# MLP products by Strassen's scheme, with operands and block sums through DRAM, in a hybrid decoder step

## The reference, cut to what matters

```python
z = rmsnorm(x, g_pre_mix) @ w_in            # attention and recurrence follow from z
mix = concatenate([attn, o], -1) @ w_out    # 1024 x 1024
x = x + rmsnorm(mix, g_post_mix)
hid = square(relu(rmsnorm(x, g_pre_mlp) @ w_up))    # w_up 1024 x 4096
x = x + rmsnorm(hid @ w_down, g_post_mlp)           # w_down 4096 x 1024
```

## Time and profile before

| | |
|---|---|
| span of the profiled execution | 4277.1 us |
| median of the runs less that span | 1.6 us |
| PE busy | 3791.6 us, 89% |
| DVE busy | 2761.0 us, 65% |
| ACT busy | 2042.7 us, 48% |
| POOL busy | 381.2 us, 9% |
| everything ahead of the last stage | 0 to 2503 us |
| `attend_prompt` | 2006 to 2503 us |
| last stage, `output_and_mlp` | 2506 to 4277 us |

### The profile page before, as it was taken

The page is one execution under the profiler, slowest core; times in us unless marked ns, Lnnn a source line. Parts: engine busy times, 40 slices in busy tenths (PEclk is TensorE's granted clock), DMA queues, the critical chain, the costliest instruction groups (busy, mean ns, idle before and its releaser), DMA issues. The chain is left out here.

```text
span 4277.1 us, 52892 instructions
## 1 busy us (share of the span) xinstructions
PE 3791.6 (89%) x18920; PEld 3002.3 (70%) x18921; DVE 2761.0 (65%) x4534; ACT 2042.7 (48%) x3270; POOL 381.2 (9%) x390
## 2 busy tenths in 40 slices
PE   8999996779776589854999989999999999999998
PEld 7878775667555245432888877888888888877776
DVE  6686566888888798787788855434544454445444
ACT  3333324556677599875777742233223322331233
POOL 0000003545210111100100000000000000000000
PEclk9999998999877799985999999999999999999999
DMA  6555444225100344334111033323333342323222
GB/s 166 172 149 167 127 125 119 89 83 161 53 20 17 104 170 171 127 101 114 53 43 36 16 124 114 91 96 94 125 122 94 109 138 92 98 79 100 71 77 69
DMA packets 283783, 435.67 MB, mean 102 GB/s; under 512 B 86136, under 2 KB 154712, under 8 KB 275224
## 3 DMA queue, kind: packets, MB, share of 16 engines
q1 hardware_dynamic: 261256, 318.98, 25.3%
q0 software_dynamic: 21872, 113.52, 7.5%
q10 hardware_dynamic: 416, 0.02, 0.0%
HBM read 371.02 MB, written 61.43 MB: 101 GB/s over the span
## 5 line engine op out<-in xcount | busy, mean ns | idle before, releaser
L3140 DVE TENSOR_TENSOR weight_parts<-weights,weight_parts 128x1024 fp32r<-128x1024 f32 x280 | 344.9, 1233 | 769.3 <-ACT weight_parts L2939 769.3
L2939 ACT ACTIVATE weight_parts<-weights 128x1024 fp32r<-128x1024 f32 x280 | 296.0, 1059 | 976.5 <-PE acc L3517 460.7
L3517 PE MATMUL acc<-act_T,weight_parts 128*128 128x512 f32 x3072 | 707.8, 392 | 9.4 <-DVE act_T L3146 7.9
L3517 PEld LDWEIGHTS acc<-act_T,weight_parts 128*128 128x128 f32 x3072 | 580.6, 189 | 133.5 <-DVE act_T L3146 6.0
L3549 PE MATMUL acc<-weight_parts,hidden_parts 128*128 128x512 f32 x2304 | 522.7, 389 | 0.0
L3549 PEld LDWEIGHTS acc<-weight_parts,hidden_parts 128*128 128x128 f32 x2304 | 432.4, 188 | 89.8
L712 PE MATMUL accumulated<-hT,w_in_parts 128*128 128x512 f32 x1536 | 355.1, 390 | 0.0
L2651 DVE TENSOR_SCALAR_CACHE_REDUCE junk_dve<-score,candidate 128x2048 bf16<-128x2048 f32 (+6 forms) x224 | 328.5, 1505 | 8.8 <-DVE candidate L2637 8.2
L712 PEld LDWEIGHTS accumulated<-hT,w_in_parts 128*128 128x128 f32 x1536 | 287.0, 188 | 60.3
L2574 ACT ACTIVATE junk_act<-score,candidate 128x1920 bf16<-128x1920 f32 (+6 forms) x224 | 285.8, 1286 | 20.7 <-DVEq L2638 15.3
L330 ACT ACTIVATE w_in_parts<-w_in_raw 128x1024 fp32r<-128x1024 f32 (+1 forms) x112 | 113.6, 1014 | 307.8 <-PE accumulated L708 121.8
(11 more groups left out here) (502 smaller groups left out, 6915.0 us busy)
## 6 DMA issues: line engine op xcount, KB each, us to landing
weights<-in_w_up SPq DMA_DIRECT2D x128, 512.0 KB
weights<-in_w_down SPq DMA_DIRECT2D x128, 512.0 KB
w_in_raw<-in_w_in SPq DMA_DIRECT2D x80, 512.0 KB, 4.1
weights<-in_w_out SPq DMA_DIRECT2D x24, 512.0 KB
w_in_raw<-in_w_in SPq DMA_DIRECT2D x64, 128.0 KB, 2.7
q_rows<-scratch_qT SPq DMA_DIRECT2D x64, 128.0 KB, 3.6
qi_rows<-scratch_qiT SPq DMA_DIRECT2D x56, 128.0 KB
x_sb<-in_x_prompt POOLq DMA_DIRECT2D x3, 2048.0 KB, 9.3
```

The lines of the kernel that those rows point to most:

```text
L2939: act.activation(w2[:, w, 0, :], raw[:, b[0], :], ACT.Copy).then_inc(hi_rdy, 1)
L3140: dve.tensor_tensor(w2[:, w, 1, :], raw[:, b, :], w2[:, w, 0, :].bitcast(F32), ALU.subtract).then_inc(lo_rdy, 1)
L3517: mm = pe.matmul(acc[:, u % nb, :], w2[:, c % 2, b, k2 * ST + n * P:k2 * ST + (n + 1) * P], aT[:, a, 2 * kk + k2, :], start=(kk == 0 and k ...
```

## The change

`attend_prompt` gets a second job for POOL: 32 times it loads 1 MB of w_down (16 times) or w_up (16 times), forms four block sums of 128x512 each and stores them (1 MB) to DRAM, spread over the tiles from the fifth on (`WITH_TILE`). `output_and_mlp` is replaced by three stages.

`output_projection` takes 16 prompt tiles of 128 rows and the sample rows as a 17th: transposes, 48 matmuls, norm, residual, second norm, transposes back. It stores the residual rows, the transposed normed rows and, by POOL, their four block sums, to DRAM.

`mlp_up` takes two halves of 1024 tokens. In Strassen's scheme (the form with 7 products and 15 sums) a product of 2 x 2 blocks takes seven block products instead of eight. A unit is a pair of 128-column blocks of w_up: 7 products of 12 matmuls; there are 32 units, 2688 matmuls. The x operands (28 pieces of 256 KB for each half) and the weight operands (7 pieces of 256 KB for each unit) come from DRAM in pieces of 128x512 through 12 buffers. DVE adds the products out of PSUM, squares, POOL forms the sums of the hidden blocks for `mlp_down`, and SP stores 7 tensors of 256 KB for each unit, in runs of 512 bytes.

`mlp_down` has 2 x 7 x 4 = 56 steps of 48 matmuls (2688). A step loads 1 MB of hidden operand (POOL's queue) and converts it in two halves; a product (four steps) needs 16 weight pieces of 256 KB, which are loaded through four buffers and converted during its predecessor's last step. The sample rows' whole MLP is done here, as 128 pieces of weight (64 up, 64 down), two buffers deep: the high and low parts of the 64 rows stand side by side as one stationary operand of 128 columns, so a piece takes two matmuls, 256 in all, and a small product with `fold` adds the two halves.

"The last block as three blocks" means that a stage has taken the place of each part of it. `newton`, the conversion and `PASSES` are as before. Cut to what the prediction speaks of (new code in the four functions):

```diff
 def attend_prompt(nc, io, sc):
+        WITH_TILE = [0, 0, 0, 0, 1, 1, 2, 2, 2, 3, 3, 3, 4, 4, 4, 3]
+                def load_weights(c):
+                    if c >= 2:
+                        pool.wait_ge(sums_out[c % 2], 16 * (c // 2))
...
+                    pool.dma_start(t, src).then_inc(w_in[c % 2], 16)
+                def weight_sums(c):
+                    pool.wait_ge(w_in[c % 2], 16 * (c // 2 + 1))
...
+                        pool.tensor_tensor(s1, a21, a22, ALU.add).then_inc(sums_rdy, 1)
+                        pool.tensor_tensor(s3, a11, a21, ALU.subtract).then_inc(sums_rdy, 1)
+                    if 0 < c < 2 * FPAIRS - 1:
+                        load_weights(c + 1)
...
+                        pool.tensor_tensor(s2, s1, a11, ALU.subtract).then_inc(sums_rdy, 1)
+                        pool.wait_ge(sums_rdy, 4 * c + 3)
+                        pool.tensor_tensor(s4, a12, s2, ALU.subtract).then_inc(sums_rdy, 1)
...
+                    pool.dma_start(dst, wsum[:, (2 * c + 1) % 3, :].rearrange("p (s d) -> p s d", s=4)).then_inc(sums_out[c % 2], 16)
                 for i in range(NT):
                     b = i % 2
                     pool.wait_ge(q_hi, i + 1)
                     pool.tensor_tensor(qs[64:P, b, :, :], qr[64:P, b, :, :], qs[64:P, b, :, :].bitcast(F32),
                                        ALU.subtract).then_inc(q_lo, 1)
...
+                    for c in range(sum(WITH_TILE[:i]), sum(WITH_TILE[:i + 1])):
+                        weight_sums(c)
-def output_and_mlp(nc, io, sc):
+def output_projection(nc, io, sc):
...
+            def _(dve):
+                for n in range(TILES + 2):
+                    if n + 1 < TILES:
+                        mix_low(n + 1)
+                    if n >= 2:
+                        turned_out(n - 2)
...
+                    y = mean_and_root(n, 0, pt)
+                    dve.scalar_tensor_tensor(z, z, y, gpm[0:pt, :], ALU.mult, ALU.mult).then_inc(scaled, 1)
...
+                    dve.tensor_tensor(x, x, z, ALU.add).then_inc(x1_rdy, 1)
+                    y = mean_and_root(n, 1, pt)
...
+                    dve.tensor_scalar(hr[0:pt, n % 2, :], x, y, None, ALU.mult).then_inc(hr_rdy, 1)
+            def _(pe):
+                for n in range(TILES + 2):
+                    if n + 1 < TILES:
+                        turn_mix(n + 1)
+                    if n < TILES:
+                        pe.wait_ge(mix_lo, n + 1)
...
+                    if n >= 2:
+                        turn_rows(n - 2)
+def mlp_up(nc, io, sc):
+    RAW, SLOTS, AHEAD, BANKS = 12, NPROD, 5, 8
...
+                for n in range(-AHEAD, len(ready_at)):
+                    while n + AHEAD < len(ready_at) and done < ready_at[n + AHEAD]:
+                        low(done)
+                        done += 1
+                    if n >= 0:
+                        out_of_bank(n)
...
+                        for q in range(QUADS):
+                            for b, a in PASSES:
+                                mm = pe.matmul(acc[:, n % BANKS, :], wp[:, n % SLOTS, b, q * P:(q + 1) * P], XC[:, i, a, q, :],
+                                               start=(q == 0 and (a, b) == (0, 0)), stop=(q == QUADS - 1 and b == 1))
+def mlp_down(nc, io, sc):
+    A_RING, B_RAW, S_RING = 4, 4, 2
+    PERSTEP = 6
+    AFTER = (3, 5, 8, 10, 13, 15)
...
+                def load_b(m):
+                    if m >= B_RAW:
+                        sp.wait_ge(b_lo, m - B_RAW + 1)
...
+                def load_w(y):
+                    if y >= S_RING:
+                        sp.wait_ge(w_lo, y - S_RING + 1)
...
+                def a_high(s):
+                    for x in range(2):
+                        g = 2 * s + x
+                        act.wait_ge(a_in[g % A_RING], 16 * (g // A_RING + 1))
+                        if s >= 2:
+                            act.wait_ge(done, s - 1)
+                        act.activation(ap[:, g % A_RING, 0, :], araw[:, g % A_RING, :], ACT.Copy).then_inc(a_hi, 1)
...
+                for s, (h, i, r) in enumerate(STEPS):
+                    if s + 1 < len(STEPS):
+                        a_low(s + 1)
+                    if s:
+                        out_of_bank(s - 1)
+                        for n, h_, second, r_ in finished(s - 1):
+                            norm_rows(k, x_no, second, r_)
+                            k, x_no = k + 1, x_no + 1
+                    if r == LAST and (h, i) != (HALVES - 1, NPROD - 1):
+                        for kp in range(FPAIRS):
+                            b_low((NPROD * h + i + 1) * FPAIRS + kp)
+                    for y in sample_pieces(s):
+                        w_low(y)
...
+                    for kp in range(FPAIRS):
+                        x, j = divmod(kp, 8)
+                        g = 2 * s + x
+                        if j == 0:
+                            pe.wait_ge(a_lo, g + 1)
+                        if r == FIRST:
+                            pe.wait_ge(b_lo, (NPROD * h + i) * FPAIRS + kp + 1)
+                        for a, b in PASSES:
+                            mm = pe.matmul(acc[:, s % BANKS, :], ap[:, g % A_RING, a, j * P:(j + 1) * P], wp[:, kp, b, :],
+                                           start=(kp == 0 and (a, b) == (0, 0)), stop=(kp == FPAIRS - 1 and a == 1))
...
+                        if kp in AFTER and AFTER.index(kp) < len(pieces):
+                            sample(pieces[AFTER.index(kp)])
```

More of the change, by code:

```diff
@@ new lines, in tokens, with load_x1 @@
+                def tokens(h, second, r):
+                    t = (8 * h + 4 * second + r) * P
+                    return slice(t, t + P)
+                order = [row for s in range(len(STEPS)) for row in finished(s)]
+                def load_x1(k):
+                    if k >= 2:
+                        pool.wait_ge(y_rdy, k - 1)
+                    n, h, second, r = order[k]
+                    pool.dma_start(x1[:, k % 2, :], sc["x1"][tokens(h, second, r), :]).then_inc(x1_in[k % 2], 16)
@@ L2931, in _ @@
+                for s in range(len(STEPS) - 2, len(STEPS)):
+                    for _ in finished(s):
+                        store(k)
+                        k += 1
+                pool.wait_ge(s_y, 1)
+                pool.dma_start(flat(io["y_sample"]), zb[0:SR, :]).then_inc(y_out, 16)
+                pool.wait_ge(y_out, 16 * (NT + 1))
             @block.scalar
             def _(act):
-                def hi(g, b, w, first=False):
-                    act.wait_ge(w_in[b[0]], b[1])
-                    if not first:
-                        act.wait_ge(w_used, g - 1)
-                    act.activation(w2[:, w, 0, :], raw[:, b[0], :], ACT.Copy).then_inc(hi_rdy, 1)
```

1538 lines of the change are left out of this document (782 added, 756 removed).

## The result

The changed kernel takes 4375.65 us (4367.65 to 4384.96, 4 runs) against 4282.51 us of the kernel before on the same chip: 1.022 times its time (95% interval 1.020 to 1.024). It is slower by 93 us, where 4239 was forecast. The profiled execution has a span of 4383.2 us, 146 us above the forecast's sum of 4237. It is the longest of the four (4384.96), 9 us above their median; what is added up from the trace is therefore held against 4383, and what edits gain against 4375.65.

A forecast was written before the change was run, and what follows sets the result against it. Matmuls on TensorE were taken as the bound, 896 fewer saving 203 us. Start 2506.1 plus output_projection 256, mlp_up 643 and mlp_down 832 gave 4237 against a span of 4277.1, so median 4239; range 4150 to 4300.

The forecast's parts named there:

- Rival E: Whole kernel: the trace after could show the full count of matmuls; the diff's loops exclude it; no chance given.
- A: Rival, mlp_down: TensorE waits 2.35 us per sample step but keeps 2.4 GHz; 4197 us, chance 0.15.
- B: Rival, mlp_down: no waits at sample pieces, conversions being done ahead of the step; 93 us go, 4146, chance 0.13.
- D: Rival: POOL too slow, 14 us rounds in attention cost 23 us, locks in all three stages as much again; 4285, chance 0.12.
- the cover: Attention: POOL's added rounds of about 10.2 us delay q_parts without cost; cover gone at 12.1 us.
- a sum that other slices reach: Attention: the extra 64 MB at 160 GB/s, beside 16 to 53 GB/s in slices 20 to 23, was taken as attainable.
- the locks: output_projection: DVE steps held by POOL's sums, 1.5 us over the cover on eight tiles, 12 us.
- a lead: mlp_up, second half's start: lead of five products against a lag of 13 us, priced at 4 us.
- The later pieces come in time up to 3.6 us a load: mlp_down sample steps: pieces after the first cause no wait while a load takes at most 3.6 us.
- rival C: mlp_down: slow loads through shallow rings; above 3.1 us each microsecond costs 39, above 3.6 another 44; 4292 at 4.0, chance 0.15.
- the wait that I did put in: mlp_down: TensorE waits 2.35 us for the first sample piece, behind DVE's subtractions and eviction, in each of 22 steps.
- The clock term: mlp_down: after each 2.35 us wait the granted clock falls, adding 1.9 us in each of 22 sample steps.

The follow-up runs named there:

- outdve: Changed kernel with output_projection's four block sums made by DVE instead of POOL, and mlp_up's conversions six products ahead instead of five: 4373.52 us.
- upstore: Changed kernel with SP issuing mlp_up's seven stores of a unit two products later in its queue: 4370.54 us.
- bring6: Changed kernel with six instead of four raw buffers for mlp_down's next-product weights, room from the sample's x rows: 4333.93 us.
- nosample: Changed kernel without the sample rows' MLP (no pieces loaded, converted or multiplied, no norm) and with two raw hidden-operand halves instead of four: 4165.01 us.
- cand2: Changed kernel with four piece and six weight buffers, first two pieces converted ahead, norm after weight conversions, attention's first loads and row stores moved: 4182.71 us.
- ring6: Changed kernel with six raw and three converted sample-piece buffers instead of two and two, and two raw hidden-operand halves instead of four: 4382.16 us.
- araw2: Changed kernel with only the hidden operand's raw halves cut from four to two: 4425.15 us.

## Why the prediction was wrong, step by step

The sum was 4237, the span 4383.2. The 146 us lie here:

| step | forecast | measured | |
|---|---|---|---|
| all before output_projection | 2506.1 | 2517.9 | +11.8 |
| output_projection | 256 | 272.0 | +16.0 |
| mlp_up | 643 | 655.2 | +12.2 |
| mlp_down, entry | 11 | 15.6 | +4.6 |
| its first step | 18 | 20.0 | +2.0 |
| sample steps, beyond matmuls (folds in) | 98 | 159.7 | +61.7 |
| changes of product and the rest | 38 | 68.8 | +30.8 |
| end | 10.5 | 17.3 | +6.8 |

**The count of matmuls and their price** were right: 896 went, and steps without waits take 10.88 us, units of `mlp_up` 19.04. Rival E is out. So are A and B: the waits were there and the half-clock stretches too. D has its locks (10 us in output_projection) but not its slow rounds in attention.

**Attention: the cover held, another thing cost.** POOL's operations took 1.26 to 1.30 us as estimated from the earlier trace rows, and `q_parts` of tiles 12 and 15 began at 2288.6 and 2416.3, 127.7 us apart, the same as in the earlier trace rows. The subtractions of the earlier trace rows are unchanged (659/689/695). But the stage is 8.2 us longer (499.6 to 507.8, first DMA to first DMA). Nearly all of it (7.9) is there by the fourth tile's `q_parts`: POOL issues its first two 1-MB loads where the stage's own first loads are under way, and TensorE waited 8.55 us. The step "a sum that other slices reach" looked at the average of slices, not at the stage's start. Issued two tiles later they gave 4 us back, and the wait at that place is gone; the other 3.9 us moved with the loads, to the fifth and sixth `q_parts`. The 3.6 us that are left of the 11.8 arose before this stage, in code that is the same; other executions had it at 2005.1 to 2014.2.

**output_projection: the locks were right, the tail was not.** 12 us were put down for locks; four tiles were 10 over. The tail after the last tile's start was taken as 27.4 and took 37.9: POOL's sums for the last tile end at 2782.5 and their stores and the stage's close at 2789.9, and the sum had none of it. By `outdve` these sums are 3 us of the 10.5; the rest was not taken apart. The first two tiles were 6 us late, while w_out was being loaded.

**mlp_up: a lead was taken where an order decided.** The first unit was 6.9 over (6.5 forecast), the second half's start 14.7, not 4. 10.5 of it is SP's order, shown by `upstore`.

**mlp_down: the later waits were put at nothing.** "The later pieces come in time up to 3.6 us a load" is the step that failed: TensorE waited 52.1 us for later pieces, of the 61.7 that these steps are over the forecast. This is rival C's mechanism. The condition was right, but the loads did not meet it: a load takes 2.7 us when alone, below the 2.9 of the earlier trace rows, and 5.3 to 7.8 behind a megabyte on another queue. A median (2.8 for these loads) hides that; rival C, which worked with one time for all, gave 4292 at 4.0 us, and chance 0.15 was too little. At the same time the wait that I did put in was too long for most steps: instead of 2.35 us the first half's first waits are 0.69 to 2.86 in ten of its eleven sample steps, 1.6 in the mean. ACT began the next operand 0.2 us before the step's first matmul in most steps of the second kind (1.0 in the step shown), and DVE's two subtractions ended 3.3 us after it, not 3.8. The second waits of these ten steps are 1.1 to 4.6, 2.6 in the mean. Three steps had a row norm ahead of the piece, which the sum gave only to the changes of product: their first waits are 8.06 to 9.09, and their excess is 38 us in all. So the sum of all first waits, 58.5 us against a forecast of 52, is near it by luck.

The clock term was right in kind, though 9 of the 14 half-clock stretches came at the second wait. Its ground was weaker than it read: besides the waits that the prediction names, the last stage of before had two of 2.30 us (at 3175.1 and 3581.5) that no half-clock stretch followed.

**Changes of product:** one round of four loads was priced at 4.5 us; with landings of 4.1 and 3.6 (medians of `down_raw`, block sums and plain blocks) the ten plain changes cost 3.3 us each instead of 1, the three with norms 9, 8.5 and 14 instead of 5.2. `bring6` shows the ring, `nosample` that pieces have no part in it.

**End:** the last store went out at 4372.8 and the span ended at 4383.2; before, 4272.8 and 4277.1. The forecast took the old distance, but the store was now on POOL's queue, and what followed was this instruction of POOL's sequencer (line, engine, operation, ns, start):

```profile
L3341 POOLq DRAIN  x1: 5601/5601/5601, 4376.7 to 4376.7; - x1
```

In `cand2`, where SP makes the last two row stores, POOL's DRAIN of 5.44 us began at 4173.4, before SP's last store at 4176.6, and the span ended 3.7 us after that store.

The range, 4150 to 4300, was too narrow by its own rule: C's price was stated for 4.0 us, while nothing in the trace of before bounded the landing behind other queues' traffic at 4.

## What to carry to other kernels

Where a pipeline is cut into short stages with shallow rings, write down for each ring the round (issue to landing under the traffic of that moment, plus conversions) against the demand in that round; two buffers are two rounds per step, and no median of loads tells it. Room for a deeper ring is not free: taken from a neighbour, it moved the wait (ring6, araw2) until both had enough. The same change was a loss of 2.2% and, with four and six buffers and several orders changed, a gain of 2.8%; count what stands ahead of each store and load in its queue before you count bandwidth.

## What the runs showed of the hardware that I had not expected

- A 256-KB load landed 2.7 us after its issue (median of the later pieces of a step), or 5.3 to 7.8 in 18 of 22 steps for the piece that had two 512-KB loads of another queue issued 1 to 2 us before it.
- POOL and DVE hold each other. A one-column DVE operation of 0.16 us took 0.58 and 1.21 beside POOL's sums, and POOL's sum of 1.64 to 1.68 us (31 times) took 7.69 while DVE went from one operation to the next without a gap (7.70 in `upstore`); that DVE held it there is read from this coincidence, and no run shows it apart. The Trainium skill (SBUF — State Buffer, SBUF: two separate sides) has the pair of ports locked by whoever starts first, for a whole instruction; that agrees with the DVE side, and the 7.69 is several DVE instructions long, which the sentence does not say.
- After a final store on POOL's queue the span went on for 10.4 us (4372.8 to 4383.2), of which 5.6 were POOL's DRAIN; after SP's in the kernel before it went on for 4.3.
